# Raw and split weight chunks taken in turns within each expert of a mixture-of-experts loop

## What is computed

```python
logits = (ht @ w_router + b_router)
top_vals, top_idx = lax.top_k(logits, TOP_K)     # 4 of 32 experts for each row
gates = jax.nn.softmax(top_vals, axis=-1)
...
gu = xblk @ w_gate_up[e] + b_gate_up[e]          # 1024 -> 2048
gate = jnp.minimum(gu[:, :D_EXPERT], SWIGLU_LIMIT)
up = jnp.clip(gu[:, D_EXPERT:], -SWIGLU_LIMIT, SWIGLU_LIMIT)
act = gate * jax.nn.sigmoid(SWIGLU_ALPHA * gate) * (up + 1)
...                                              # act @ w_down[e] + b_down[e], 1024 -> 1024
```

## Time and profile before

| | us |
|---|---|
| median of 3 runs | 1842.84 (1841.66 to 1843.86) |
| the profiled execution | 1843.58 |
| its span | 1841.9 |
| expert pairs in it, 15 | 1070.6 |
| TensorE matmuls busy | 1622.8, 88% of the span |
| VectorE busy | 1069.8, 58% |
| ScalarE busy | 780.4, 42% |
| mean transfer rate over the span | 269 GB/s |

### The profile page before, as it was taken

One profiled execution on the slowest core, in us unless ns is written; L12 is line 12 of the kernel. 1 busy time (PEld: TensorE's weight loads), 2 busy tenths in 40 slices (PEclk: granted clock), 3 DMA queues, 4 the chain that ended last, 5 costly groups with the idle time before them and its releaser, 6 DMA issues. The chain is left out here.

```text
span 1841.9 us, 22633 instructions
## 1 busy us (share of the span) xinstructions
PE 1622.8 (88%) x7599; PEld 1098.3 (60%) x7600; DVE 1069.8 (58%) x1418; ACT 780.4 (42%) x996; POOL 286.3 (16%) x348
## 2 busy tenths in 40 slices
PE   6988968989889789879889898898899799998998
PEld 3555455645645546536546546456476368887996
DVE  5466654643654645546536536446478757887663
ACT  5353312442533533524424425325365644436541
POOL 0140420110010010011001000100143200004420
PEclk9998969899989999999999998998999899999999
DMA  6123828898999998998999999999997622211001
GB/s 211 40 82 124 318 86 332 340 416 347 364 411 351 365 391 348 412 366 343 414 359 356 422 354 369 402 358 360 411 377 291 223 88 69 92 46 69 1 24 46
DMA packets 107661, 496.42 MB, mean 270 GB/s; under 512 B 22817, under 2 KB 40846, under 8 KB 57330
## 3 DMA queue, kind: packets, MB, share of 16 engines
q1 hardware_dynamic: 97554, 474.02, 65.2%
q0 software_dynamic: 10048, 21.64, 3.5%
HBM read 476.60 MB, written 19.02 MB: 269 GB/s over the span
## 5 line engine op out<-in xcount | busy, mean ns | idle before, releaser
L2023 DVE TENSOR_TENSOR part<-ring,part 128x2048 fp32r<-128x2048 f32 x138 | 313.8, 2296 | 253.9 <-ACT part L1579 253.9
L1579 ACT ACTIVATE part<-ring 128x2048 fp32r<-128x2048 f32 x136 | 256.6, 1911 | 217.2 <-DMA ring<-in_w_down 181.6
L1823 PE MATMUL bank<-part,actT_hi 128*128 128x512 f32 x544 | 175.0, 450 | 95.6 <-DVE rest L2047 86.6
L1767 PE MATMUL bank<-part,xT_hi 128*128 128x512 f32 x816 | 214.2, 406 | 35.9 <-DVE part L2023 35.9
L1767 PEld LDWEIGHTS bank<-part,xT_hi 128*128 128x128 f32 x816 | 153.9, 193 | 72.0 <-DVE part L2023 37.2
L1823 PEld LDWEIGHTS bank<-part,actT_hi 128*128 128x128 f32 x544 | 119.5, 223 | 126.6 <-DVE part L2023 89.8
L1795 PE MATMUL bank<-ring,rest 128*64 128x512 f32 x720 | 164.8, 596 | 6.8 <-DMA ring<-in_w_gate_up 5.2
L2023 DVE TENSOR_TENSOR part<-rest,part 128x2048 fp32r<-128x2048 f32 x64 | 147.3, 2305 | 17.7 <-ACT part L1579 15.9
L1579 ACT ACTIVATE part<-rest 128x2048 fp32r<-128x2048 f32 x64 | 120.6, 1908 | 11.2 <-DMA rest<-in_w_down 9.2
L1767 PE MATMUL bank<-part,xT_lo 128*128 128x512 f32 x408 | 114.5, 404 | 0.0
L1795 PEld LDWEIGHTS bank<-ring,rest 128*64 128x64 f32 x720 | 49.1, 137 | 106.4 <-issue 84.1
(11 more groups left out here) (554 smaller groups left out, 2801.7 us busy)
## 6 DMA issues: line engine op xcount, KB each, us to landing
ring<-in_w_gate_up SPq DMA_DIRECT2D x194, 1024.0 KB, 9.9
ring<-in_w_down SPq DMA_DIRECT2D x66, 1024.0 KB, 8.5
rest<-in_w_gate_up SPq DMA_DIRECT2D x62, 1024.0 KB, 10.7
rest<-in_w_down SPq DMA_DIRECT2D x62, 1024.0 KB, 8.8
ring<-in_w_in SPq DMA_DIRECT2D x14, 1024.0 KB, 5.0
rest<-in_w_ada SPq DMA_DIRECT2D x8, 1536.0 KB, 6.7
ring<-in_w_out SPq DMA_DIRECT2D x16, 512.0 KB, 5.9
expert_rows<-rest SPq DMA_DIRECT2D x16, 512.0 KB, 7.6
```

Of the source, the lines that this page charges most:

```text
L1579: nc.scalar.activation(hi[part], raw_slot(m, slot), ACT.Copy).then_inc(sig("hi_ready"), counts)
L1767: ins = nc.tensor.matmul(bank[g][:], rows[:, c, :], w[:, g * 512:(g + 1) * 512], start=first, stop=last, skip_group_check=True)
L1823: ins = nc.tensor.matmul(bank[6 + g][:], rows[:, n, :], w[:, k, g * 512:(g + 1) * 512], start=first, stop=last, skip_group_check=True)
L2023: V.tensor_tensor(lo[part], raw_slot(m, slot), hi[part].bitcast(F32), ALU.subtract).then_inc(sig("lo_ready"), counts)
```

## The change

Chunks are taken, loaded and put into slots in a new order. In a small turn: S0 S1 S2 S3 D8 S4 S5 D9 S6 S7 D10 D11. In a big turn: G0 G1 G2 R8 G3 G4 R9 G5 G6 G7 R10 R11. The n-th load of a turn goes to slot n % 6. The stores go behind the ninth load. The lists are made in bank 3 in a small turn and in bank 7 in a big one, one chunk or two earlier. The rows of the next expert are turned ahead of the last two down chunks. On ScalarE the split of D8 goes ahead of `copy_act`, those of D10 and D11 ahead of the small sigmoid, and `copy_act_small` ahead of the split of G3; on VectorE the split of D8 goes ahead of `act_lo`, that of D10 ahead of `index_small`, and the splits of G0 and G1 behind `gated_small`, `times_gate_small` and `rows_lo`.

```diff
+    SMALL_TURN = (0, 1, 2, 3, 8, 4, 5, 9, 6, 7, 10, 11)
+    BIG_TURN = (0, 1, 2, 8, 3, 4, 9, 5, 6, 7, 10, 11)
...
+            def wait_big(j, n):
+                c = BIG_TURN[n]
+                if c < 8:
+                    wait_lo(sp, first(j) + 4 + c)
+                else:
+                    wait_raw(sp, j, c)
...
             def rest_of_big(j, e, before):
-                for c in range(SLOTS, CHUNKS):
-                    wait_lo(sp, first(j) + 4 + c - SLOTS)
-                    load_chunk(sp, a, m, e if c < 8 else before, c, c % SLOTS)
...
+                for n in range(SLOTS, CHUNKS):
+                    wait_big(j, n - SLOTS)
+                    load_nth(BIG_TURN, n, e, before)
+                    if n == 8:
                         store_big(j)
...
                 nc.scalar.activation(spare[0:1, 0:1], con(m, "ident", 1)[0:1], ACT.Sigmoid)
+                hi_of_pair(j, 0)
                 copy_act(j + 1)
-                hi_of_pair(j, 0)
-                hi_of_pair(j, 1)
+                for s in (1, 2, 3):
+                    hi_of_pair(j, s)
                 sigmoid_small(j)
-                hi_of_pair(j, 2)
-                hi_of_pair(j, 3)
...
                 hi_of_pair(j, 6)
+                copy_act_small(j)
                 hi_of_pair(j, 7)
-                copy_act_small(j)
...
+                list_next(i, 3)
+                wait_actT(j + 1)
+                pe.wait_ge(sig("y_ready"), i + 1)
+                pe.wait_ge(sig("index_ready"), i + 2)
+                small_down(j, 8)
+                next_small(j, 4)
                 biases_small(i)
-                next_small(j, 4)
-                list_next(i)
-                for c in (5, 6, 7):
-                    next_small(j, c)
-                wait_actT(j + 1)
+                next_small(j, 5)
+                small_down(j, 9)
+                next_small(j, 6)
+                next_small(j, 7)
                 turn_rows(i + 1)
-                pe.wait_ge(sig("index_ready"), i + 3)
-                for c in range(8, CHUNKS):
-                    down(first(j) + c - 8, c - 8, c)
+                small_down(j, 10)
+                small_down(j, 11)
...
+                pe.wait_ge(sig("index_ready"), i + 2)
                 first_gate_ups(first(j) + 4, (4, 5), j + 2, [("act_small", j + 1)])
                 turn_act_small()
-                for c in (2, 3):
-                    gate_up(first(j) + 4 + c, c - 2, c)
+                big_gate_up(j, 2)
+                pe.wait_ge(sig("y_ready"), i + 1)
+                if more:
+                    list_next(i, 7)
+                pe.wait_ge(sig("actT_small"), j + 1)
+                down_small(j, 8)
+                big_gate_up(j, 3)
                 biases(i)
-                gate_up(first(j) + 8, 2, 4)
-                if more:
-                    list_next(i)
+                big_gate_up(j, 4)
+                down_small(j, 9)
+                for c in (5, 6, 7):
+                    big_gate_up(j, c)
...
+                down_small(j, 10)
+                down_small(j, 11)
...
+                lo_of_pair(j, 0)
                 act_lo(0, j + 1)
                 act_lo(1, j + 1)
-                for s in (0, 1):
-                    lo_of_pair(j, s)
+                lo_of_pair(j, 1)
+                lo_of_pair(j, 2)
...
-                for s in (2, 3):
-                    lo_of_pair(j, s)
+                lo_of_pair(j, 3)
                 clip_small(j)
+                gated_small(j)
+                times_gate_small(j)
+                rows_lo(j + 2)
                 lo_of_pair(j, 4)
-                gated_small(j)
-                rows_lo(j + 2)
                 lo_of_pair(j, 5)
-                times_gate_small(j)
...
-                for s in (6, 7, 8):
+                for s in (6, 7, 8, 9):
                     lo_of_pair(j, s)
-                index(2 * j + 4)
-                for s in (9, 10, 11):
+                index(2 * j + 4, 7)
+                for s in (10, 11):
                     lo_of_pair(j, s)
```

128 lines of the change are left out of this document (63 added, 65 removed).

## The result

| | before | changed |
|---|---|---|
| median of 5 runs, us | 1843.86 (1841.66 to 1846.11) | 1829.83 (1824.02 to 1832.63) |
| ratio, 95% interval | | 0.9917 (0.9895 to 0.9940) |
| profiled execution, its span | 1843.58, 1841.9 | 1824.02, 1822.4 |
| 14 pairs, per pair | 70.8 | 69.4 |

The change makes the kernel faster by 14 us or 0.8%, where 69 us were forecast. Between the two profiled executions it is 19.5 us of span. The page of the changed kernel: TensorE's row of part 1, and of the slices the granted clock and the DMA share, which answers to the earlier trace rows.

A forecast was written before the change was run, and what follows sets the result against it. Neither engine was full: two TensorE stops and their clock loss stretched 58.6 us of work to 71.4 a pair. Changed: 58.6 + 4.8 + 2.6 + 0.8 = 66.8, saving 4.6 fifteen times, 69 us: 1774 us, range 1730 to 1835.

The forecast's parts named there:

- the case of a faster kernel: Whole kernel: the change makes it faster, chance 0.82; likeliest time 1774 us.
- more stops stay: Rival: late landings make further TensorE stops with clock loss, 69.3 to 71.1 us a pair, 1812 to 1839 us; chance 0.15.
- changes from raw to split: On TensorE: switching between chunk kinds taken as 0, bound 0.3 us at each of some eight, 2.4 us a pair.
- The lists: Making the lists earlier removes 4.3 us a pair before G5 and 2.4 us of the wait before D8.
- Stop (a): Before G5: TensorE waits 2.6 us for VectorE's index, plus about 1.7 us of clock; all 4.3 us go.
- The pair and the number of pairs: Expert loop: 15 pairs of 71.4 us, each getting 4.6 us shorter, 69 us in all.
- D8: Start of the down chunks: landed at 66.2 to 67.4 us, with 0.8 us of stop counted before it.
- The walk: Following one changed pair through landings, splits and TensorE's work: 66.2 to 67.4 us, taken as 66.8.
- G0: At `first_gate_ups`: TensorE stops 4.8 us for VectorE's splits behind D11, plus 2.6 us of clock loss.
- `copy_act_small` ahead of the split of G3: On ScalarE: delays the split of G3, which VectorE still finishes at 43.1 us, in time; cost nothing.
- The hole: In the transfers near 710 us, DMA share 0.26: no loads issued during VectorE's index; to go with the stop before G5.
- The rule on the memory's 358 GB/s: Sign against the change: HBM transfers bound at about 358 GB/s per core, an estimated 74.9 us a pair, no gain.

The follow-up runs named there:

- c4: Kernel before with only the big expert's list moved to bank 7 after G2, its index behind the split of G5: 1782.2 us.
- a1: Kernel before with both lists made earlier in banks 3 and 7, order of chunks, loads and splits unchanged: 1765.8 us.
- b3: Changed kernel with VectorE's split of G0 back between clip and gate, that of G1 ahead of the product: 1830.2 us.
- b2: Changed kernel with the small turn back in the old order, also on ScalarE and VectorE; only the big turn interleaved: 1789.0 us.
- b1: Changed kernel with the big turn back in the old order; only the small turn interleaved: 1854.2 us.
- d4: Changed kernel's lists, `copy_act_small` order and late stores, with plain chunk order on engines but D8 loaded four chunks before use: 1836.6 us.
- c2: Kernel before with the lists alone, plus products with the rounded part first at D8, G0 and G1: 1753.7 us.
- c3: Kernel before with the lists alone, plus ten unused products on TensorE ahead of turning the rows before D8: 1783.0 us.
- c1: Changed kernel with products with the rounded part first at D8, G0 and G1: 1788.5 us.
- a3: Changed kernel with D8 one raw chunk later, behind S4, but the wait for the activations' remainder left ahead of S4: 1834.7 us.
- a0: The changed kernel itself, run again as a base beside the kernel before: 1822.5 us.
- e1: Changed kernel with R8 loaded behind G3 instead of G2, loads and slots only, TensorE's order unchanged: 1823.3 us.

## Why the prediction was right in sign and wrong in size

The time lies in the range of 1730 to 1835 us, at its top, and the case of a faster kernel held. But 14 us came where 69 were forecast. The number fits the rival "more stops stay", which I gave 0.15; its 69.3 to 71.1 us a pair hold the 69.4 measured. That is in part luck: that rival expected late landings by the row gather or a store, and what came is D8's own stop and the changes from raw to split. By the steps:

- **The lists, right.** Stop (a) was priced at 4.3 us a pair; c4 measured 4.3 (70.8 to 66.5). With the small list, 6.7 were counted, and a1 measured 5.5 (70.8 to 65.3): part of the earlier index is waited off for D8's split.
- **The pair and the number of pairs, wrong.** 71.4 us was one stretch cut into 15 equal windows, not 15 pairs. In the trace the first pair takes 64.6 us and the 13 behind it 71.3 in the mean, 70.8 over all 14; what follows the 14th stayed the same within 1.6 us. The first pair had no 4.6 us to give, and went to 66.4. Counted like this, 15 x 4.6 = 69 becomes 14 x 4.0 = 56 us.
- **D8, wrong.** The walk gave it a stop of 0.2 to 1.4 us and took 0.8, with no clock loss. It has 2.9 us and 1.8 us of clock in the pair shown, and 2.7 us of stop in the mean (37.4 / 14). The landing takes 6.0 to 7.2 us and not 4.9 to 6.1, and D8's time at the full clock was carried on to all that follows it: S4 is used later, and so D11 is loaded and split later.
- **G0, right in mechanism, its stop smaller.** 4.8 us and 2.6 of clock were forecast, 3.5 and 2.6 came. TensorE does wait for VectorE's chain behind D11, as written. That the order within this chain matters is not so: b3 undid it and nothing was won.
- **Changes from raw to split, wrong.** Taken as 0, with a bound of 0.3 us a change; b2 shows 1.2 us a pair for the four changes of the big turn at an equal clock and nearly equal stops. The changed kernel has eight more than before.
- **`copy_act_small` ahead of the split of G3, "costs nothing".** TensorE indeed hardly waits for G3. But the walk looked at TensorE alone: G3's slot stays taken, from a landing at 758.9 until 770.7, and in b1 and d4 this order makes a stop. What it costs the changed kernel is open.
- **The transfers, as feared.** The hole stayed, at another place, with 382 GB/s where about 400 were to be seen. SyncE's waits for R8 are the longest kind, as written.

From 69 us to the 19.5 between the two profiled executions it is so: 13 us by the pair and the number of pairs, and 14 x (69.4 - 66.8) = 36 us by the walk. The sum of the walk was 58.6 + 7.4 + 0.8 = 66.8 us. In the pair shown, from one D8 to the next (732.00 to 802.16), it is about 59.8 of work, 6.2 at G0 and 4.2 at D8 (1.8 of clock, and 2.4 of stop ahead of the next), 70.2 us; the mean of 14 is 69.4, since the stops and the clock behind them differ from pair to pair.

The larger fault lies ahead of these. The walk followed the two parts of the change together and never priced the lists alone. My own numbers had them: 71.4 - 4.3 - 2.4 = 64.7 us, against 66.8 us for the whole. By them interleaving costs 2.1 us a pair. I called its terms a gain. Measured, the rest of the change costs 3.9 (69.2 - 65.3).

The rule on the memory's 358 GB/s (the Trainium skill, DMA: Bandwidth & Descriptors, section Bandwidth) was cited without its condition: the same section gives that figure for two cores streaming at once, and up to 425 GB/s for one core alone. This kernel runs on one core, and the trace agrees with the second: c2's pairs run at 410 GB/s on their whole length.

**What interleaving does**, as far as the runs show it. In the plain order TensorE takes four down chunks and then the gate and up chunks, each for 2.7 us, while ScalarE and VectorE split one in 1.9 and 2.3 us; after one stop at D8 the splits run ahead of it, and the slower clock behind that stop is covered (c3). In the changed order the landing and splitting hold TensorE a second time, at G0, with a fall of the clock that isn't covered. Waiting for one splitting step less there takes 34 us off the interleaved order (c1) and, with D8, 12 off the plain one (c2). At D8 the changed order never got this edit in a form that works, and the order with D8 behind S4 was never run without a3's stray wait.

Of the other 35 us the changes on TensorE are some 16 if only the big turn's are counted at b2's price, and some 33 if the four more of the small turn cost the same. TensorE's busy time says 2.0 us a pair, 28 us (61.6 in c1 against 59.6 in c2), with a clock of 0.97 against 0.99 in it. So they can be most of what is left, but a run that separates them from the clock and from `copy_act_small` is missing. That order on ScalarE is the rival that stands untested: it is in a0 and in every run with interleaved turns, and not in a1, c2, c3 and c4.

## What to carry to other kernels

Where a change has two parts, price each alone from the same rows before walking them together; here one gave 78 us and the other took back 57. In this ring of six slots it was better to group the chunks that need preparation than to spread them. Let the consumer start with the part that is ready first, which gave 12 us in the plain order and 34 in the interleaved, and look in the trace whether another wait ahead of it undoes the edit (c1 at D8). A slowed clock is to be tested before it is blamed: preventing it in one place only moved it to another (c3). And before an edit that frees a buffer is read as a test of the wait, look which buffer the engine waits for afterwards: in e1 it was another one, for as long.

## What the runs showed of the hardware

- A load of 1 MB that went out when all earlier ones had landed took 4.7 to 5.0 us to land (G7, in 13 pairs of the changed kernel). One that went out 1.4 to 1.7 us before the last of four earlier ones had landed took 6.0 to 7.2 us (D8 there), and in a1, where three or more were on their way, 9.0 to 13.2 us (D8 to G1).
- A raw float32 chunk with 64 columns of weights takes 1.73 us in a row of its kind and 1.87 us alone between split ones, and the chunk behind it 2.9 to 3.0 instead of 2.72.
- Ten products (2.60 us together) in a stop of 3.9 us kept the granted clock up; what followed took 2.82 us instead of 5.20. Behind the next stop, of 3.2 us, the clock fell in 8 of 13 pairs.
- One core sustained 410 GB/s over 14 pairs, 900 us, with the DMA engines busy all of the time.
